# GpSimd's long element-wise operations in parts, the causal mask inside the first weighted sum, and a key norm's epsilon on GpSimd, in a hybrid decoder step

## What is computed

```python
q, k, v, ga, qi, wi, ki, ub, gb, uc, gc = project(hp, pos_p, norm_g[l], w_in[l], q_norm_g[l], k_norm_g[l])
att = prompt_sparse_attention(q, k, v, qi, wi, ki, topk_p)      # top 132 of the admissible keys
pool, pool_st = pool_branch(ub, ...)                            # windows 2, 4, 8, 16: mean minus token
conv, conv_st = conv_branch(uc, ...)                            # depthwise, 31 taps, LayerNorm, swish
hp = hp + merge_groups(att, ga, pool, gb, conv, gc, w_out[l])

def indexer_scores(qi, wi, ki):                                 # which keys a query may use
    dots = jnp.einsum('bqhd,bsd->bqhs', qi, ki).astype(jnp.float32) * (D_IDX ** -0.5)
    w = wi.astype(jnp.float32) * (N_IDX_HEADS ** -0.5)
    return jnp.einsum('bqh,bqhs->bqs', w, jax.nn.relu(dots))
...
sc = jnp.where(adm[None], sc, -jnp.inf)                         # adm: key position <= query position
_, idx = lax.top_k(sc, top_k)
```

## Time and profile before

| | |
|---|---|
| median of 3 runs | 785.02 us |
| all runs | 785.02, 784.52, 794.11 us |
| the profiled execution | 793.32 us, span 792.0 us |
| mean granted TensorE clock over the span | 0.963 |

### The profile page before, as it was taken

One profiled execution on the slowest core, in us unless ns is written; L12 is line 12 of the kernel. 1 busy time (PEld: TensorE's weight loads), 2 busy tenths in 40 slices (PEclk: granted clock), 3 DMA queues, 4 the chain that ended last, 5 costly groups with the idle time before them and its releaser, 6 DMA issues. The chain is left out here.

```text
span 792.0 us, 13109 instructions
## 1 busy us (share of the span) xinstructions
PE 728.0 (92%) x4628; PEld 595.4 (75%) x4628; DVE 542.2 (68%) x1342; ACT 326.3 (41%) x840; POOL 272.0 (34%) x305
## 2 busy tenths in 40 slices
PE   4899999899798998999998999998978899899998
PEld 3897656578787896777998856565877788677888
DVE  3538897899897975434535789789999788632232
ACT  3725455434745432323131554533465643322202
POOL 1013887822745510011110458783255552000000
PEclk9999999999888999999999999999999899999999
DMA  5543040304121635014024404022422254401302
GB/s 184 162 117 111 5 146 14 107 33 135 54 84 54 196 125 188 1 54 150 1 86 117 141 3 142 23 62 65 142 61 53 61 170 150 161 1 54 105 2 108
DMA packets 54977, 71.87 MB, mean 91 GB/s; under 512 B 12977, under 2 KB 30585, under 8 KB 54881
## 3 DMA queue, kind: packets, MB, share of 16 engines
q1 hardware_dynamic: 54802, 70.96, 28.6%
q10 hardware_dynamic: 111, 0.08, 0.0%
HBM read 64.05 MB, written 7.61 MB: 90 GB/s over the span
## 5 line engine op out<-in xcount | busy, mean ns | idle before, releaser
L1188 PE MATMUL R<-x_hi,W_r 128*128 128x268 f32 x448 | 140.7, 314 | 9.1 <-DVE bufA L1531 5.1
L1201 PE MATMUL R<-yT,W 128*128 128x268 f32 (+2 forms) x768 | 131.3, 329 | 8.5 <-DVE yT L1531 8.5
L1190 PE MATMUL R<-x_hi,W_r 128*128 128x268 f32 x448 | 135.7, 303 | 0.0
L1189 PE MATMUL R<-x_lo,W_r 128*128 128x268 f32 x448 | 135.2, 302 | 0.0
L1172 PE MATMUL R<-W_r,x_hi 128*128 128x512 f32 (+3 forms) x320 | 123.9, 387 | 9.5 <-DVE W_r L1531 9.5
L1201 PEld LDWEIGHTS R<-yT,W 128*128 128x128 f32 x768 | 112.6, 199 | 25.5 <-DVE yT L1531 9.3
L1173 PE MATMUL R<-W_r,x_hi 128*128 128x512 f32 (+3 forms) x320 | 119.6, 374 | 0.0
L1174 PE MATMUL R<-W_r,x_lo 128*128 128x512 f32 (+3 forms) x320 | 119.1, 372 | 0.0
L1188 PEld LDWEIGHTS R<-x_hi,W_r 128*128 128x128 f32 x448 | 92.0, 205 | 19.0 <-issue 10.3
L788 POOL TENSOR_TENSOR W_r<-W,W_r 128x1024 fp32r<-128x1024 f32 x28 | 66.8, 2397 | 96.5 <-ACT W_r L897 96.4
L1189 PEld LDWEIGHTS R<-x_lo,W_r 128*128 128x128 f32 x448 | 92.3, 206 | 0.5 <-issue 0.5
(11 more groups left out here) (250 smaller groups left out, 1266.3 us busy)
## 6 DMA issues: line engine op xcount, KB each, us to landing
W<-in_w_in SPq DMA_DIRECT2D x52, 512.0 KB, 4.6
KV<-in_cache_k SPq DMA_DIRECT2D x32, 256.0 KB, 3.1
W<-in_w_out SPq DMA_DIRECT2D x8, 1024.0 KB, 6.9
KV<-in_cache_v SPq DMA_DIRECT2D x32, 256.0 KB, 4.0
ubx<-qkv_rows SPq DMA_DIRECT2D x16, 256.0 KB, 4.3
W<-in_w_in SPq DMA_DIRECT2D x8, 296.0 KB, 3.3
out_new_k_prompt<-kz SPq DMA_DIRECT2D x8, 256.0 KB, 2.3
out_new_v_prompt<-V SPq DMA_DIRECT2D x8, 256.0 KB
```

What stands on the lines that cost most here:

```text
L1188: pe.matmul(out, hi[:, cols], x_hi[:, kc, toks], start=(kc == 0), stop=False)
L1189: pe.matmul(out, hi[:, cols], x_lo[:, kc, toks], start=False, stop=False)
L1190: m = pe.matmul(out, lo[:, cols], x_hi[:, kc, toks], start=False, stop=(kc == KC - 1))
L1201: m = pe.matmul(R[:, k, 0:hi - lo], W[:, slot(x), kc % 4, 128 * (u[1] % 4):128 * (u[1] % 4) + 128], yT[:, kc, lo:hi], start=(kc == 0), sto ...
```

## The change

Three things. On GpSimd the subtraction of a low part is issued as four instructions of 256 columns, the two widest pooling sums as two of half the width, and each key product as two of 256 columns; the semaphore counts up with the last part. The epsilon of the key and query norms is added by GpSimd; the factor 1/64 moves into ScalarE's squares by way of a second set of row factors, `rinv_hd`, which VectorE writes once a layer. The causal triangle goes into the first head's weighted sum: the columns ahead of the tile's own keys are weighed as before, those of its own keys are weighed and get the triangle in one instruction. The last causal step after the selection remains for tile 1 alone.

```diff
             def rest(m):
                 pool.wait_ge(*hi_s.at(m + 1 - AHEAD))
-                lo2_s.did(pool.tensor_tensor(w_raw(m, W_r), w_raw(m), w_high(m, W_r).bitcast(F32), ALU.subtract))
+                for x in range(4):
+                    per = GROUPS[LOADS[m][0]][3]
+                    part = (slice(None), x * per // 4, slice(None) if per == 4 else slice(256 * (x % 2), 256 * (x % 2) + 256))
+                    done = pool.tensor_tensor(w_raw(m, W_r)[part], w_raw(m)[part], w_high(m, W_r)[part].bitcast(F32), ALU.subtract)
+                lo2_s.did(done)
...
+                pool.wait_ge(*kss_s.at(n + 1))
+                kq_mid.did(pool.tensor_scalar(kss[0:r, n % 2, :], kss[0:r, n % 2, :], EPS, None, ALU.add))
                 pool.wait_ge(*kq_mid.at(n + 1))
...
-            ps_s.did(pool.tensor_tensor(bufA[:, :, 1:n], ubx[:, :, 1:n], ubx[:, :, 0:n - 1], ALU.add))
+            for c in range(2):
+                done = pool.tensor_tensor(bufA[:, c, 1:n], ubx[:, c, 1:n], ubx[:, c, 0:n - 1], ALU.add)
+            ps_s.did(done)
...
-                    kp_s.did(pool.tensor_tensor(KV[:, n % 4, :], KV[:, n % 4, :], qb[:, b % 2, :], ALU.mult))
+                    for x in (0, 256):
+                        done = pool.tensor_tensor(KV[:, n % 4, x:x + 256], KV[:, n % 4, x:x + 256], qb[:, b % 2, x:x + 256], ALU.mult)
+                    kp_s.did(done)
...
-                evA.did(act.activation(ksq[0:r, n % 2, :], R[0:r, bank(u), :], ACT.Square, scale=rinv[0:r, i:i + 1]))
+                evA.did(act.activation(ksq[0:r, n % 2, :], R[0:r, bank(u), :], ACT.Square, scale=rinv_hd[0:r, i:i + 1]))
...
-                    pe.wait_ge(*acc_s.at(first if first <= IX_1 else first + 2))
+                    pe.wait_ge(*acc_s.at(first))
...
             dve.wait_ge(*rinv_s.at(1))
+            dve.tensor_scalar(rinv_hd[0:SR, 0:NT], rinv[0:SR, 0:NT], HD ** -0.5, None, ALU.mult)
...
-                dve.wait_ge(*kss_s.at(n + 1))
-                kq_mid.did(dve.tensor_scalar(kss[0:r, n % 2, :], kss[0:r, n % 2, :], 1.0 / HD, EPS, ALU.mult, ALU.add))
...
                 if h == 0:
-                    acc_s.did(dve.tensor_scalar(dst, src, w, None, ALU.mult))
+                    k = min(hi, START[i]) - lo
+                    done = dve.tensor_scalar(dst[:, 0:k], src[:, 0:k], w, None, ALU.mult)
+                    if hi == WIDTH[i]:
+                        done = stt(dst[:, k:hi - lo], src[:, k:hi - lo], w, tri[0:ROWS[i], 0:ROWS[i]], ALU.mult, ALU.add)
+                    acc_s.did(done)
...
-                if k > 2 * n + 1:
+                if k > 2 * n + (i == 1):
                     return
...
-            def piece(p):
-                gather(p)
-                if p in (IX_1 - 1, len(PIECES) - 1):
-                    dve.wait_ge(*acc_s.at(acc_s.n))
-                    for i in (1, 2) if p == IX_1 - 1 else (3, 4):
-                        causal(i, acc_s)
```

More of the change, by code:

```diff
@@ L141 @@
 K_END = K_SUM + 4
-ACC_END = len(PIECES) + 4
+ACC_END = len(PIECES)
 GATES = [(u, {"ub": 2, "gc": 6, "ga": 0}[u[0]] + u[1]) for step in PLAN for u in step
@@ L319, in program @@
         lnv = small[:, 90:98]
+        rinv_hd = small[:, 90:98]
         lnr = small[:, 98:106]
@@ L851, in pool_layer @@
             n = POOL_STATE + NTOK
-            ps_s.did(pool.tensor_tensor(bufA[:, :, 1:n], ubx[:, :, 1:n], ubx[:, :, 0:n - 1], ALU.add))
+            for c in range(2):
+                done = pool.tensor_tensor(bufA[:, c, 1:n], ubx[:, c, 1:n], ubx[:, c, 0:n - 1], ALU.add)
+            ps_s.did(done)
             pool.wait_ge(*ps_s.at(1))
-            ps_s.did(pool.tensor_tensor(bufB[:, :, 3:n], bufA[:, :, 3:n], bufA[:, :, 1:n - 2], ALU.add))
+            for c in range(2):
+                done = pool.tensor_tensor(bufB[:, c, 3:n], bufA[:, c, 3:n], bufA[:, c, 1:n - 2], ALU.add)
+            ps_s.did(done)
             pool.wait_ge(*ps_s.at(2))
@@ L1598, in gather @@
                 last[i, lo] = acc_s.n
-            def causal(i, s):
-                d = area(i, SENT + START[i], SENT + WIDTH[i])
-                s.did(dve.tensor_tensor(d, d, tri[0:ROWS[i], 0:ROWS[i]], ALU.add))
             steps_of, mark, slot_of = {1: 0, 2: 0, 3: 0, 4: 0}, {}, {1: 3, 2: 0, 3: 1, 4: 2}
@@ L1624, in select @@
                 elif k == 2 * n + 1:
-                    causal(i, tk_s)
+                    d = area(1, SENT + START[1], SENT + WIDTH[1])
+                    tk_s.did(dve.tensor_tensor(d, d, tri, ALU.add))
                 elif k % 2 == 0:
@@ L1696, in vector_layer @@
                 for x in range(0, IX_K, 2):
-                    piece(p)
-                    piece(p + 1)
+                    gather(p)
+                    gather(p + 1)
                     p += 2
@@ L1877, in vector_layer @@
                     if i and h == 0:
-                        assert steps_of[i] == 2 * (LOW_ROUNDS if i == 1 else ROUNDS) + (3 if i == 1 else 2)
+                        assert steps_of[i] == 2 * (LOW_ROUNDS if i == 1 else ROUNDS) + (3 if i == 1 else 1)
                         dve.wait_ge(*tk_s.at(mark[i]))
```

## The result

The changed kernel took 784.86 us (median of 20 runs, 779.09 to 787.88), the kernel before on the same chips 788.18 us (20 runs, 784.52 to 796.24). The ratio is 0.995, with a 95% interval of 0.9929 to 0.9971 (it compares the fast runs and is not the quotient of the two medians): a gain of 3.9 us (2.3 to 5.6), not the forecast 8, which the interval leaves out. The profiled execution after has a span of 784.6 us. The two profiled executions lie 7.4 us apart, twice the gain: the one before took 793.32 us, 5.1 above its median, the one after 785.88, 1.0 above. So a ledger read from this pair explains more than was gained, above all in its terms for the clock.

What follows compares the result with a forecast made beforehand. VectorE was taken to set the time from 166 to 210 us. Terms of 3.35 us a layer, 6.7 for both, plus 1.2 for the clock gave 7.9 us: 777 us from the median, range 768 to 787.

Steps and rivals of the forecast that it cites:

- (e): 64-row addition at 219.34 us: again held to the train's end, now 0.8 us longer; -0.7 us a layer, bounds -0.8 and +1.2.
- (a): End of the key units, gap 1.42 us: VectorE's saved instructions gain 0.8 us a layer, bounds 0 and 1.4.
- The new wait of 0.6 us: Before the first key transpose: longer GpSimd work stalls TensorE for a new 0.6 us, taken to lie within the 1.42 us gap.
- (b): End of the query units, gaps 1.77 and 1.55 us: epsilon and last causal pair removed from VectorE gain 0.4 us a layer.
- the case that the collision moved away: End of the query units: at most 1.8 us if VectorE's weight steps no longer stood behind the key norm's L829 and L831.
- (c): First attention steps, gap 2.4 us ahead of the first channel mean: removing L1602 gains 2.25 us a layer, bounds 1.0 and 2.4.
- (d): Gap of 0.85 us at 218.04: the held gate product waits only for a quarter subtraction; gain 0.7 us, bounds 0.3 and 0.85.
- the clock, +0.6: After the first channel mean: TensorE's fall to 1.2 GHz may stay out, counted half; 0.6 us a layer, 1.2 in all.
- The prices on GpSimd: A 256-column subtraction part about 0.73 us, the small epsilon operation 0.3 us, each split key product +0.15 us.
- everything lets go: Rival: the parts also free the 64-row addition and the clock falls stay out; 13.9 us gain, 771 us; chance 0.23.
- The gaps only move: Rival: key and query gains are lost at the next ScalarE wait, half the channel-mean gain remains; some 3 us, 782; chance 0.2.
- the slower rival: VectorE gets in at no seam between parts, so its two-operand instructions wait for GpSimd's whole queue; 789 us; chance 0.07.

Runs made afterwards that it cites:

- with the wait: Changed kernel, with GpSimd waiting for its two layer-norm powers to complete before the eight subtraction parts of loads 26 and 27: 773.65 us, ratio 0.9799.
- before with the wait: Kernel before, with only GpSimd's wait for its two layer-norm powers ahead of the subtractions of loads 26 and 27 added: 787.47 us, ratio 0.9979.
- the freed versions: Changed kernel with GpSimd's wait for its powers (773.65 us), one 128-row power (775.04), the two powers swapped (774.26), or the second power on all rows (776.52).
- The pair of 24 and 128 rows: Changed kernel, second layer-norm power on 24 rows (784.86 us), against the same with that power on all 128 rows (776.52 us, ratio 0.9845).
- the other three cures: Changed kernel with GpSimd's wait for its two powers (773.65 us), one power of 128 rows by 5 columns (775.04), or the two powers swapped (774.26).

## Why the prediction was wrong

The step that failed is (e): a term of -0.7 us for a hold whose full price, once the rest of the change had made everyone earlier, was 3 to 4 us a layer in the profile. The sum was 3.35 us a layer and 1.2 for the clock. By its steps:

- **(a), end of the key units, +0.8: wrong, +0.07.** The saved instructions went into waits of VectorE for ScalarE's relu (0.86, 0.27 and 1.34 us between 97 and 106 us, of which before had only one of 0.17), so VectorE reached the residues no earlier. The step looked for the limit at the gap and not for VectorE's waits on the way to it. The new wait of 0.6 us came, at 0.68 (and 0.67 in the second layer), and added to the delay instead of lying within the gap.
- **(b), end of the query units, +0.4: mis-sized.** The bound that I named for the case that the collision moved away, 1.8, is what happened: 3.32 us of gaps became 1.55, so 1.77. It is the extra instruction for the epsilon on GpSimd that moves most of it, as the run with the epsilon alone shows (second gap 0.56), and the parts move the rest. The gap of 0.74 us at the first scores, which no step named, shrank by 0.47. I had counted that instruction against the key path and not against this collision.
- **(c), first channel mean, +2.25: right in place, 1.86 in size** (2.41 to 0.55). With the splits alone the gap is 0.78, with the causal edits alone 0.35: the gap was a collision, and either part of the change removes most of it.
- **(d), the gap at the powers, +0.7, and the clock, +0.6: both wrong, right together by luck.** The product was not freed: it takes 1.24 us instead of 1.41 and the next one 0.68 instead of 0.44, and the gap grew from 0.85 to 1.24. What was won is in TensorE's busy time, 1.6 us between the mean and the powers, as the fall of the clock at 206.5 us stayed out. Together 1.25 us (5.41 to 6.66), where the two terms say 1.3; 1.2 in the second layer.
- **(e), the 64-row addition, -0.7: right mechanism, the price is the step that failed.** I took the hold to last 0.8 us longer, and it did (5.93 against 5.20 us, now on the third of the four additions and not on the second). But I priced only the lengthening. The hold as a whole had cost little before, a gap of 0.60 us in this layer and 1.18 in the other, since TensorE was late enough itself. At the powers TensorE is 6.7 us earlier, and it needs 0.9 less for the work up to the gap; VectorE behind the hold is only 5.3 earlier (its last addition starts at 220.94, before at 226.23). So the gap grew by 2.29 us. In the first layer the clock adds 1.7: its level is low for 10.2 us from the powers to the place at 239 us, where it was for 5.5. In the second it is 3.4 in both, and the loss is idle time alone: the gap grew from 1.18 to 2.88, and one of 1.05 opened at 609 us. The loss was 4.0 us in the first layer (6.66 ahead to 2.68) and 3.1 in the second. Freed, the same hold is worth 11.2 us in medians (784.86 to 773.65, from two sets of runs).
- **The clock, +1.2 in all**, was sized by one fall. What the level of 1.2 GHz can have cost over the whole span is at most (1 - 0.963) x 792.0 = 29.3 us in the profiled execution before, 20.4 after and 13.9 with the wait. In the first layer it is 1.6 us ahead of the query units' end, in no step of mine, and 1.6 ahead of the powers, where I had 0.6. The execution before lies 5.1 us above its median, so how much of this is the change's stays open. The gaps are firmer: up to the mean they agree within 0.03 us between the profile of before and that of before with the wait, while the clock's level around the powers is low for 6.8 us in one and for 3.4 in the other.

The prices on GpSimd came out: 740 ns for a part (0.73 forecast), 0.33 us for the small operation (0.3). A key product in halves costs 0.25 us more, not 0.15.

The rival "everything lets go" (13.9 us of gain) is what the freed versions do (12.6 to 16.3 us in medians); in the change as it stands its condition was not met. What I held against it, that one seam had let VectorE in and another of the same kind had not, is answered by what stands ahead of the two trains in the earlier trace rows: the first follows a wait for GpSimd's own result, the second the 24-row power. "The gaps only move" had some 3 us of gain, and 3.9 were measured: it was nearest to the number. It was right on (a), wrong on (b) and (c), and named another place than the one where the gain went. No train formed at the gate products (1.24 and 0.68 us), so the slower rival fell. The rule of the Trainium skill that I weighed in step (e) (GPSIMD Engine Reference, "2.1 Instruction dispatch": each core goes on when its own rows are done) gave the right side. The pair of 24 and 128 rows bears out what follows from it, 5.93 against 0.19 us. The profile shows GpSimd as one engine, so the cores themselves were not seen.

## What to carry to other kernels

Before pricing a saved wait, follow the engine that gains to its next hold: a term that costs little because everyone is late costs in full once they are not. Splitting long GpSimd instructions pays only if VectorE can get in at the seams. See that the last instruction ahead of a back-to-back run works on all 128 rows, or that GpSimd waits for its own last result; then the splits and the freed time gained 2% here, where neither the splits nor the wait alone gained anything measurable.

## What the runs showed that I had not expected

- One instruction of GpSimd on 24 rows in place of 128, ahead of a run of eight, costs a VectorE instruction 5.7 us and the kernel some 8 us of 785 (784.86 against 776.52, from two sets of runs; the other three cures gain 10 to 11).
- A short full-row instruction behind it (1.14 us, 128 x 4) undoes this, with no wait.
- A collision can stretch either engine: at the end of the query units it is GpSimd's product now (1.96 against 1.16 us), and TensorE does not wait for it there.
- Splitting a whole subtraction of 2397 ns into four of 740 ns, which overlap a little, costs 0.44 us of GpSimd's busy time each (79.1 us for the 28 against 66.8). The only wait of TensorE for it that I found is the 0.7 us ahead of the first key transpose.
